# Diagonals built on ScalarE, context selection by blocks, and the second query block's norm inside the first head pair, in a two-layer hybrid transformer step

## The reference

```python
h = x * (1.0 + sc1) + sh1
hq, hff, hfb, hi, hg, aq, ak, av, ga, gb = split(h @ w_in)
o_rec = hgrn2_branch(...)                      # bidirectional gated scan, 8 heads
q, k = rms_norm(aq, q_g), rms_norm(ak, k_g)    # 16 query heads, 4 key heads of 64
# latent q and k are rotated (axial rotary); context reads context only,
# latent tokens read latent keys and 128 cached context keys
o_att = softmax(q k^T / 8) v
y = sigmoid(ga) * (o_rec @ w_branch_rec) + sigmoid(gb) * (o_att @ w_branch_att)
x = layer_norm(alpha * x + g1 * (y @ w_out))
h2 = x * (1.0 + sc2) + sh2
# PEER: 8 heads; per head two sets of 128 sub keys
s = einsum(h2 @ w_query, sub_keys)             # (token, head, 2, 128)
s_top, i_top = top_k(s, 16)
cand = s_top[..., 0, :, None] + s_top[..., 1, None, :]      # 256 candidates
best_s, best_pos = top_k(cand, 16)
expert = i_top0 * 128 + i_top1                 # of the chosen candidate, 16384 experts
gate = softmax(best_s)
a = gelu(einsum('td,thkd->thk', h2, u_tab[expert]))         # 128 rows of 1024 a token
x = layer_norm(alpha * x + g2 * einsum('thk,thkd->td', gate * a, v_tab[expert]))
```

## Time and profile before

| | |
|---|---|
| runs, median (lowest to highest) | 6030.76 us (6028.83 to 6032.37) |
| the profiled execution | 6079.51 us, its span 6077.7 us |
| granted TensorE clock, mean | 0.937 |
| busy: PE, PEld, DVE, ACT, POOL | 83%, 45%, 62%, 14%, 29% of the span |
| HBM read in the span | 1581 MB |

### The profile page before, as it was taken

How to read it: one execution, slowest core, us unless ns; L and a number is a source line. 1 busy time by engine, 2 the same in 40 slices (tenths; PEclk the granted TensorE clock), 3 DMA queues, 4 the chain that set the end, 5 groups by cost and what they waited for, 6 DMA issues and landing times. The chain is left out here.

```text
span 6077.7 us, 62226 instructions
## 1 busy us (share of the span) xinstructions
PE 5025.4 (83%) x18696; PEld 2730.3 (45%) x18696; DVE 3743.5 (62%) x7541; ACT 825.2 (14%) x2126; POOL 1738.9 (29%) x1567
## 2 busy tenths in 40 slices
PE   7998888897877777777689988988969777777776
PEld 4886467543432222222258854675434322322222
DVE  0664432478788787866606644325787777878665
ACT  1121132100111001010112211321011110100100
POOL 0000000065544444443300000001655444444433
PEclk9998899998999999999999988999989999999999
DMA  3110113497899999999821111134977999999997
GB/s 136 46 47 34 57 56 133 148 378 297 329 382 406 410 403 415 394 418 421 352 99 44 37 35 60 64 141 167 379 293 302 383 409 407 404 413 399 418 421 327
DMA packets 251840, 1589.80 MB, mean 262 GB/s; under 512 B 28848, under 2 KB 38704, under 8 KB 105648
## 3 DMA queue, kind: packets, MB, share of 16 engines
q0 software_dynamic: 221184, 1342.28, 55.0%
q1 hardware_dynamic: 15936, 224.93, 9.7%
q10 hardware_dynamic: 14448, 19.42, 0.9%
HBM read 1581.27 MB, written 5.24 MB: 261 GB/s over the span
## 5 line engine op out<-in xcount | busy, mean ns | idle before, releaser
L756 PE MATMUL banks<-arena 128*128 128x512 f32 x1152 | 652.0, 649 | 318.1 <-PEq L1233 309.0
L368 POOL DMA_INDIRECT arena<-in_peer_uv,eidx x512 | 579.4, 1132 | 754.4 <-POOLq L367 717.0
L1678 DVE SCALAR_TENSOR_TENSOR arena<-arena 128x1024 f32<-128x1024 f32 x512 | 627.1, 1225 | 143.2 <-DMA arena<-in_peer_uv,eidx 130.7
L349 POOL DMA_INDIRECT arena<-in_peer_uv,eidx x512 | 591.1, 1154 | 392.9 <-POOLq L348 254.1
L758 PE MATMUL banks<-arena 128*128 128x512 f32 x1152 | 621.8, 623 | 0.0
L422 ACT ACTIVATE late<-late 128x1 f32<-128x1 f32 (+1 forms) x1026 | 208.3, 203 | 2367.6 <-ACTq L421 2367.3
L756 PEld LDWEIGHTS banks<-arena 128*128 128x128 f32 x1152 | 198.1, 199 | 726.0 <-issue 726.0
L335 POOL COPY late<-arena 128x640 f32 x16 | 11.4, 718 | 1782.0 <-POOLq L334 1782.0
L756 PE MATMUL banks<-ring,arena 128*128 128x512 f32 x512 | 294.7, 658 | 224.8 <-PEq L1233 224.4
L837 PE MATMUL banks<-hT,ring 128*128 128x320 f32 x1536 | 432.5, 433 | 2.9 <-PEq L834 2.9
L368 POOL DMA_INDIRECT ring<-in_peer_uv,eidx x256 | 283.8, 1109 | 455.1 <-POOLq L367 431.4
(11 more groups left out here) (256 smaller groups left out, 7448.3 us busy)
## 6 DMA issues: line engine op xcount, KB each, us to landing
ring<-in_wblk SPq DMA_DIRECT2D x106, 2048.0 KB
arena<-in_peer_uv,eidx POOLq DMA_INDIRECT x1024
arena<-in_lnrows ACTq DMA_DIRECT2D x6, 1024.0 KB, 7.5
arena<-in_sk ACTq DMA_DIRECT2D x4, 1024.0 KB, 9.0
hT<-in_peer_uv,eidx POOLq DMA_INDIRECT x256
ring<-in_peer_uv,eidx POOLq DMA_INDIRECT x256
x<-in_x_sample ACTq DMA_DIRECT2D x1, 2048.0 KB, 18.2
late<-in_state ACTq DMA_DIRECT2D x32, 64.0 KB, 1.8
```

The costliest lines, as they stand in the source:

```text
L349: nc.gpsimd.indirect_dma_start(grow[j], None, ins["peer_uv"], bass.IndirectOffsetOnAxis(ap=eidx[:, n, r:r + 1].bitcast(U32), axis=0)).then ...
L368: nc.gpsimd.indirect_dma_start(gslot[j], None, ins["peer_uv"].rearrange("(e h) d -> e (h d)", h=2), bass.IndirectOffsetOnAxis(ap=eidx[:, n ...
L756: nc.tensor.matmul(banks[:, 4, :], diag[n], row[:, 0:CB], start=start, stop=stop, skip_group_check=True).then_inc(diag_used, 1)
L1678: V.scalar_tensor_tensor(u, u, 1.0, h2[:, t - 1, :], ALU.mult, ALU.mult, accum_out=av[:, r:r + 1])
```

## The change

- **ScalarE diagonals.** The vector engine's `diagonal` is gone. In tiles 1 to 4 ACT does for each row the GELU, a 128x1 copy with the gate as scale, and the diagonal, a 128x128 copy of the identity with that product as scale, with a drain between them (`row_weight`).
- **Query block 1 inside head pair 0.** The three norms are one function of seven parts. Keys and query block 0 are done before attention as before. POOL gets `qkn_pool` twice, once for pairs 0 to 3 and once for pairs 4 to 7. The seven parts of query block 1 come on DVE behind `lowest` in units 0 to 6 of pair 0; its root is made on ACT in unit 1.
- **Context selection by blocks.** ACT signals `stage_ready` after each of the four score blocks, and DVE makes both levels, the positions and the look-up of two heads for each.
- **Context norm.** The modulation is folded into the norm's gain and shift ahead of time: h2c = xn * (gain * scale) + (base * scale + shift), so h2c is made before x itself. The statistics of each half come right after its `add_branch`.
- **Loads.** After block 38 the ring goes on in slot 1, so the later blocks (25 to 38 for the latent tokens) lie in the other slot than before.

```diff
@@ SP
-                with sp.Fori(0, (B_PQ - B_MIX) // 2) as i:
+                with sp.Fori(0, (NB - B_MIX) // 2) as i:
                     for s in range(2):
-                        load(s, l * NB + 2 * i + B_MIX + s)
-                with sp.Fori(0, (NB - B_PQ) // 2) as i:
-                    for s in range(2):
-                        load(s, l * NB + 2 * i + B_PQ + s)
+                        load(1 - s, l * NB + 2 * i + B_MIX + s)
@@ POOL
-                with pool.Fori(0, QH // 4) as i:
+                with pool.Fori(0, QH // 8) as i:
...
+                pool.wait_ge(qkn_pool, 1)
+                pool.sem_inc(qkn_pool, -1)
+                with pool.Fori(QH // 8, QH // 4) as i:
@@ ACT
-                square_root(NT * 8)
                 act.wait_ge(kn_act, 1)
@@ ACT att_pair, after the exponentials of u + 2
+                        if u == 1 and before is None:
+                            square_root(NT * 8)
@@ ACT score_block of the context
                     nc.scalar.copy(stage[:, n * CB:(n + 1) * CB], banks[:, b, :]).then_inc(bank_free[b], 1)
+                    act.drain().then_inc(stage_ready, 1)
@@ ACT, tiles 1 to 4
+                def row_weight(t, r):
+                    gelu(r, r + 1)
+                    act.drain()
+                    nc.scalar.activation(wv[:, r:r + 1], av[:, r:r + 1], ACT.Copy, scale=gates[t % 2][:, r:r + 1])
+                    act.drain()
+                    diagonal(r % DIAGS, wv[:, r:r + 1])
                 for t in range(1, NT):
                     for r in range(SLOTS):
-                        gelu(r, r + 1)
+                        row_weight(t, r)
@@ DVE attention
+                def head_norm(c, heads, gain, part):
...
+                    if part == 0:
+                        dve.wait_ge(qkv_ready, 1)
+                        dve.sem_inc(qkv_ready, -1)
+                        V.tensor_tensor(a, v, v, ALU.mult)
+                    if part == 1:
+                        V.tensor_reduce(...); V.tensor_scalar(...); dve.drain().then_inc(var_ready, 1)
+                    if part == 2:
+                        dve.wait_ge(std_ready, 1)
+                        V.reciprocal(...); V.tensor_tensor(v, v, small..., ALU.mult)
+                    if part == 3: V.tensor_tensor(v, v, rows_g..., ALU.mult)
+                    if part == 4: two products with cos and sin into a
+                    if part == 5: two products with sin and cos into b
+                    if part == 6: the subtraction and the addition into v
+                for part in range(7): head_norm(1024, KV, P + HD, part)
+                for part in range(7): head_norm(0, 8, P, part)
...
+                        if u < 7 and before is None:
+                            head_norm(512, 8, P, u)
+                        if u == 6 and before is None:
+                            dve.drain().then_inc(qkn_pool, 1)
@@ DVE peer_dve
                         dve.drain().then_inc(dots_ready, 1)
-                        if r:
-                            diagonal(r - 1, gates[t % 2])
-                        elif t > 1:
-                            diagonal(SLOTS - 1, gates[(t - 1) % 2])
                         if r % 4 == 3:
@@ DVE context
+                V.tensor_tensor(rows_ctx, base, scale, ALU.mult)
+                V.tensor_tensor(shift, shift, rows_ctx, ALU.add)
+                V.tensor_tensor(scale, scale, gain, ALU.mult)
                 for h in range(2):
                     add_branch(0, h, h, bc_ctx, tmp_ctx)
-                norm_stats(0)
-                norm_apply(0, ln1_ctx, bc_ctx, h2c)
-                choose(gates[0])
+                    V.bn_stats(stats[:, 6 * h:6 * h + 6], xc[:, h * CB:(h + 1) * CB])
...
+                V.tensor_scalar(xc, xc, mv[:, 0:1], small[:, 0:1], ALU.subtract, ALU.mult)
+                V.tensor_tensor(h2c, xc, scale, ALU.mult)
+                V.tensor_tensor(h2c, h2c, shift, ALU.add).then_inc(h2_ready, 1)
+                V.tensor_tensor(xc, xc, gain, ALU.mult)
+                V.tensor_tensor(xc, xc, base, ALU.add)
+                for n in range(4):
+                    dve.wait_ge(stage_ready, 1)
+                    dve.sem_inc(stage_ready, -1)
+                    first_level(stage, 4 * n, 4 * n + 4)
+                    candidates(2 * n, 2 * n + 2)
+                    second_level(2 * n, 2 * n + 2)
+                    positions(gates[0], 2 * n, 2 * n + 2)
+                    look_up_both(2 * n)
+                expert_ids()
```

More of the change, by code:

```diff
@@ L183, in build @@
         tmp_ctx = arena[:, 20480:20992]
+        rows_ctx = arena[:, 20992:22016]
         tmp_lat = arena[:, 5120:5632]
@@ L330, in _ @@
                 pool.sem_inc(qkn_pool, -1)
-                with pool.Fori(0, QH // 4) as i:
+                with pool.Fori(0, QH // 8) as i:
+                    for b in range(2):
+                        pool.wait_ge(qst_free[b], 1)
+                        pool.sem_inc(qst_free[b], -1)
+                        nc.gpsimd.tensor_copy(qstage[b], qkv[:, :, bass.ds((2 * i + b) * P, P)]
+                                              ).then_inc(qst_ready[b], 1)
+                pool.wait_ge(qkn_pool, 1)
+                pool.sem_inc(qkn_pool, -1)
+                with pool.Fori(QH // 8, QH // 4) as i:
                     for b in range(2):
@@ L421, in gelu @@
                 act.sem_inc(dots_ready, -1)
-                nc.scalar.activation(av[:, first:last], av[:, first:last], ACT.Gelu).then_inc(gelu_ready, 1)
+                return nc.scalar.activation(av[:, first:last], av[:, first:last], ACT.Gelu)
             def diagonal(n, weight):
@@ L633, in _ @@
                 score_block(3)
-                act.drain().then_inc(stage_ready, 1)
                 exponentiate(gates[0])
@@ L1143, in _ @@
                 for n in range(KD):
[L1144 removed]
+                    s, f = (NB + n) % 2, n % 2
                     pe.wait_ge(w_full[s], 16)
@@ L1202, in _ @@
                 with pe.Fori(0, 2) as i:
-                    for s in range(2):
+                    for n in range(2):
+                        s = 1 - n
                         pe.wait_ge(w_full[s], 16)
@@ L1480, in _ @@
[L1480 to L1486 removed]
+                    if part == 0:
+                        dve.wait_ge(qkv_ready, 1)
+                        dve.sem_inc(qkv_ready, -1)
+                        V.tensor_tensor(a, v, v, ALU.mult)
+                        dve.drain()
@@ new lines, in head_norm @@
+                    if part == 3:
+                        V.tensor_tensor(v, v, rows_g[:, bass.ds(l, 1), gain:gain + HD].unsqueeze(2)
+                                        .to_broadcast([P, NT, heads, HD]), ALU.mult)
+                        dve.drain()
+                    if part == 4:
+                        V.tensor_tensor(a[:, 1:NT, :, 0:32], lat[:, :, :, 0:32], cs, ALU.mult)
+                        V.tensor_tensor(a[:, 1:NT, :, 32:64], lat[:, :, :, 0:32], sn, ALU.mult)
+                    if part == 5:
+                        V.tensor_tensor(b[:, 1:NT, :, 0:32], lat[:, :, :, 32:64], sn, ALU.mult)
+                        V.tensor_tensor(b[:, 1:NT, :, 32:64], lat[:, :, :, 32:64], cs, ALU.mult)
+                        dve.drain()
@@ new lines, in head_norm @@
+                    if part == 6:
+                        V.tensor_tensor(lat[:, :, :, 0:32], a[:, 1:NT, :, 0:32], b[:, 1:NT, :, 0:32], ALU.subtract)
+                        V.tensor_tensor(lat[:, :, :, 32:64], a[:, 1:NT, :, 32:64], b[:, 1:NT, :, 32:64], ALU.add)
+                        dve.drain()
+                for part in range(7):
+                    head_norm(1024, KV, P + HD, part)
+                dve.drain().then_inc(kn_pe, 1)
+                dve.drain().then_inc(kn_act, 1)
+                for part in range(7):
+                    head_norm(0, 8, P, part)
@@ new lines, in look_up_both @@
+                def look_up_both(h):
+                    c, one = slice(h * TOPK, (h + 2) * TOPK), slice(h * TOPK * TOPK, (h + 2) * TOPK * TOPK)
+                    spots = [y[:, one] for y in (stage, work)]
+                    keys = tif[:, 2 * h:2 * h + 4].rearrange("p (h a) k -> p h a k", a=2)
+                    for a in range(2):
+                        V.tensor_tensor(r3(spots[a], TOPK), (paf, pbf)[a][:, c].unsqueeze(2).to_broadcast([P, 2 * TOPK, TOPK]),
+                                        iota[:].unsqueeze(1).to_broadcast([P, 2 * TOPK, TOPK]), ALU.is_equal)
+                    dve.drain()
+                    for a in range(2):
+                        spot = spots[a].rearrange("p (h s k) -> p h s k", h=2, s=TOPK)
+                        V.tensor_tensor(spot, spot, keys[:, :, a, :].unsqueeze(2).to_broadcast([P, 2, TOPK, TOPK]), ALU.mult)
+                    dve.drain()
+                    for a in range(2):
+                        V.tensor_reduce((e1, e2)[a][:, c], r3(spots[a], TOPK), AX.X, ALU.add)
@@ L1772, in _ @@
                     peer_dve(t)
-                diagonal(SLOTS - 1, gates[(NT - 1) % 2])
```

99 lines of the change are left out of this document (46 added, 53 removed).

## The result

The changed kernel takes 5934.2 us, median of four runs (5927.2 to 5938.7), against 6031.6 for the kernel before (6028.8 to 6032.6). The ratio is 0.9838, with a 95% interval of 0.9821 to 0.9855: 97 us faster, where the prediction said 85 (5946, range 5912 to 5988).

A forecast was written before the change was run, and what follows sets the result against it. No one engine bounds the kernel; transfers bound most of a latent tile, pausing when DVE falls behind. Terms sum to 42.1 us a layer, 84 for both, from 6030.8 to 5946; own range 5925 to 5970, wider range 5912 to 5988.

The forecast's parts named there:

- 1. diagonals: Latent expert tiles: with diagonals on ScalarE, VectorE no longer falls behind transfers; gain 24.4 us a layer, bounds 16 and 30.
- 2. query block in the pair: Attention start: first score 18.4 us earlier, 10 given back in the first head pair; net 8.4 a layer, -3.6 to +18.4.
- 3. loads: Start of the latent mix: its first weight block is fetched 8.7 us earlier; gain 6.1 a layer, bounds 5 and 6.1.
- 4. context norm: Path to h2: two 128x1024 operations leave it and half the statistics hides; gain 3.2 us a layer, 2.6 to 3.8.
- 5. selection by blocks: Context mix: DVE's selection starts some 18.5 us earlier and ends near 1191, not 1204; gain 0.
- so -10: First head pair: time given back for the second query block's seven parts and table switches, 10 us a layer, bounds 0 and 22.
- PE doesn't wait for it: Context mix: PE needs the banks only at 1213.72, 1204.5 when shifted, after the selection's end near 1191; so gain 0.
- Rival B: Latent query stage: moved starts could close half the holes, 13.3 and some 12 us a layer; 5921 us, chance 0.08.
- A: Latent expert tiles: the gathers don't gain, pauses come from elsewhere; saves 17.7 us a layer, 5995 us, chance 0.09.
- C: Latent query holes grow or the first pair exposes all its parts: 12 to 20 us a layer less, 5980, chance 0.08.
- E: Whole kernel: the change does nothing, all freed time being waited out elsewhere; 6025 us, chance 0.02.
- D: Latent tiles: ScalarE sets the row pace, slower by 0.2% above 2.61 us a row, 6437 at 3.0; chance 0.03.

The follow-up runs named there:

- the second profile of before: The kernel before, unchanged, executed and profiled once more: 6024.6 us in one execution, span 6022.8.
- the run with the longer chain: The changed kernel with four more 128x128 multiplications and drains in ScalarE's chain of each row: 6379.0 us in one execution.

## Why the prediction was right, and where it wasn't

The total came out within 12 us. By terms, a layer:

| term | predicted | read in the traces of layer 1 | undone, timed, halved |
|---|---|---|---|
| 1. diagonals | 24.4 | 19.8 | 22.4 |
| 2. query block in the pair | 8.4 | 13.3 | 11.3 |
| 3. loads | 6.1 | 9.3 | 7.4 |
| 4. context norm | 3.2 | 4.0 | 2.3 |
| 5. selection by blocks | 0 | 0 (3.6 if undone) | 4.1 |
| sum | 42.1 | 46.4 | 47.5 |

The measured whole is 48.7 a layer, and the second profile of before gives 47.5 in layer 1. The parts add up to it as far as this can tell: each timed one is good to about 4 a layer, and the timed 4.1 of part 5 saves what part 3 would otherwise lose, so it is no gain over the kernel before. That the total is so close is in part luck: term 1 was too large and terms 2 and 3 too small.

*1, diagonals.* Right in place, a little large. The tiles came to 324.4, not 322.7: the first 16 rows of a tile still take 43 to 45 and the third 16, with the second-level pieces, 42, where 40.3 was expected for all. The reason, that VectorE falls behind the transfers in the pieces, carries some 70 to 80% of it (30.9 of 45 by the medians, 17.5 of 22.3 by the tiles). The rest is the order, late release of a row's slot, which the prediction named in half a sentence ("no longer waits for the next row's dot") and didn't price. The 1.33 of a dot measured 1.35, the 1.3 of ScalarE's row 1.12. The upper bound of 30 is a wrong sum: four tiles at the 319 that it names are 39 below the 1315 of before, which moves the 58 of all bounds to 67. The Trainium skill, "ScalarE: Activation LUTs", Rules for kernel authors, would have left the diagonals on VectorE and this term at nothing; the traces go against it at this shape and load: the diagonal takes 402 ns on ScalarE, 389 to 415 on VectorE, and moving it was worth 45 us here.

*2, query block.* The earlier start is right, 18.0 (22.1 less 4.1) for 18.4. The mis-sized step is "so -10": 3.0 was given back in the pair, which took 38.7 and not "some 45", and 1.8 in the next. A step of 4.7 against 3.55 over seven steps counted PE's and DVE's work as if each step waited for the other in full. The windows of the kernel before, 714 to 735 and 736 to 750, and of the one after, 693 to 714, 714 to 721 and 742 to 750, show what it left out:

```profile
714.00:735.00 21.00, 20.38 (x112) 13.06 (x112) 5.53 (x8) 6.51 (x15) 0.03 (x1) 0.53 0.00 1
...
736.00:750.00 14.00, 13.10 (x81) 9.68 (x79) 4.42 (x6) 5.57 (x12) 0.72 (x1) 1.00 0.42 150
```
```profile
693.00:714.00 21.00, 19.95 (x96) 12.33 (x100) 14.11 (x12) 8.81 (x16) 0.00 (x0) 0.51 0.05 18
...
714.00:721.00 7.00, 6.55 (x62) 4.62 (x50) 5.74 (x5) 2.03 (x5) 0.00 (x0) 1.00 0.72 263
...
742.00:750.00 8.00, 6.21 (x23) 4.49 (x24) 1.65 (x2) 2.58 (x5) 0.00 (x0) 0.65 0.01 2
```

After the wait the granted clock is 0.53 and 0.51, the lower level (1.2 GHz) nearly throughout, for the first 21 us, and then 1.00, in both kernels. In the kernel before, the pair's first steps therefore take 3.2 to 4.2 and not 3.55. Three of the seven parts lie in these 21 us: PE stays busy 19.95 of 21 while DVE does 14.11, and the half grows by 0.8 only. The other four lie at the full clock, and the half grows by 2.1. That this is why the price halved is argued from the rows, not tried. In the second pair the clock of 0.65 from 742 to 750 stands beside the longer half (20.0 against 18.2); why it fell there isn't shown.

*3 and 4.* The waits are as sized, 6.5 and 3.3. What the terms left out is PE's clock behind a wait: with the wait of 6.49 gone the first matmuls of the mix are 2.8 faster as well, and behind the shorter wait for `h2c` PE gains another 0.7.

*5, selection by blocks.* Against the kernel before the term is 0, as said: there the third mix block had no wait. But the reason, "PE doesn't wait for it", holds in the changed kernel only because the selection is split; in one piece it costs 3.6. By the prediction's numbers a selection in one piece would end 3.2 earlier than the 1203.95 of before by term 4, and "it needs the banks at 1213.72, 1204.5 when shifted", so 3.7 would be left. Two things are missing in this. The mix itself got 2.8 shorter up to there by the clock, and ScalarE needs a table load and its copies, 1185.81 to 1188.19 in the run, between DVE's end and PE. In the changed kernel PE wants the third block 56.2 behind the start of the mix, a selection in one piece ends 55.7 behind it (before: 59.0 and 49.2), and PE waits. What used up this cover is term 3, which pulls PE ahead of the selection by 6.5; terms 2 and 4 move both alike. The prediction said what it costs if the cover is gone only as "if it ended over 12 later".

*The profile's own time.* The prediction expected 5995 in a profile, carrying the 48.7 that the profiled execution had above the median over to the kernel after. It came to 5927. The step that failed is that carry. *Rival B* had priced the holes of the latent query stage as something that a kernel could gain; they were in one execution only, so there was nothing to gain, and the timed 97 doesn't contain them. *Rivals A, C and E* are out by the tiles, the pair and the idle times above, *D* by ScalarE's waits, and the run with the longer chain shows the price it would have had.

## What to carry to other kernels

In this kernel a ring of slots fed by transfers lost time when the usual stretch of its consumer (four rows and a piece, 10.5) took longer than the transfers of as many rows (10.08), and a little more when a slot was given back behind the next row's work. At 9.5 it lost next to nothing, and a single longer stretch was made good by the rows behind it. So compare stretch by stretch and not by busy shares. Where one part of a change pulls an engine earlier, price the cover of each hidden part against the shifted times, with every engine that stands between. And before a hole without a named releaser is priced, profile the same kernel twice.

## What the hardware showed unexpectedly

- One execution of the kernel before had PE idle for 24.9 us in layer 1 and 29.6 in layer 2 within the latent query stage, released by "issue"; the second profile of it had 0.3 to 0.9 at the same places.
- Drains in ScalarE's chain are cheap here: two of them with the gaps cost 0.22 beside 0.90 of work, and four more multiplications with a drain each cost 1.86, 0.465 each.
- A table switch inside the pair is a load of 1.28 and begins 0.18 after the copy before it: no drain beside it is to be seen. The Trainium skill, "ScalarE: Activation LUTs", What ACT_TABLE_LOAD costs, gives 2.66 with its drain; the trace shows the load at the length that the page has for it, and no drain.
- The granted clock fell behind short waits of PE: to 0.74 after 6.49 idle, to 0.79 after 2.30, and the 32 matmuls behind them took 16.73 and 15.67 instead of 13.9. Here such a wait cost more than its idle time.
- The end of the query projection, which no part of the change touches, lies between 683.9 and 690.0 in the 14 profiles. A stage's start read from a single profile is good to some 3 us.
